# Twelve output-gate pieces and the scan's gate projected between the steps of the triangular inverses, LayerNorm beside the scan

## What is computed

```python
z = h @ w_in
c_in, q, k, v, zg, b_raw, a_raw, gate_c, gate_d = split_cols(z, IN_SPLITS)
u = c_in[..., :512] * sigmoid(c_in[..., 512:])
u = causal_depthwise_conv(u, conv_dw_w) + conv_dw_b          # 31 taps
y_conv = silu(layer_norm(u, gain, bias)) @ w_conv_out
q, k, v = silu(causal_depthwise_conv([q, k, v], gdn_conv_w))  # 4 taps
q, k = l2_normalize(q) * 64 ** -0.5, l2_normalize(k)         # per head
o = gated_delta_rule(q, k, v, beta, g)                       # chunks; (I + L)^-1 per chunk
y_delta = (rms_norm(o, gdn_norm_gain) * silu(zg)) @ w_gdn_out
y = sigmoid(gate_c) * y_conv + sigmoid(gate_d) * y_delta
return y @ w_out
```

## Time and profile before

| | us |
|---|---|
| median of 3 runs | 907.82 |
| lowest and highest | 902.79, 908.47 |
| profiled execution, its time | 912.77 |
| its span | 911.0 |
| TensorE busy in the span | 800.3 (88%) |
| VectorE, ScalarE, GpSimd busy | 565.3, 474.7, 269.3 |
| first VN of the scan begins at | 291.53 |
| last gate piece ends, yc begins at | 427.4, 429.0 |

### The profile page before, as it was taken

The page is one execution under the profiler, slowest core; times in us unless marked ns, Lnnn a source line. Parts: engine busy times, 40 slices in busy tenths (PEclk is TensorE's granted clock), DMA queues, the critical chain, the costliest instruction groups (busy, mean ns, idle before and its releaser), DMA issues.

```text
span 911.0 us, 11270 instructions
## 1 busy us (share of the span) xinstructions
PE 800.3 (88%) x4126; PEld 615.0 (68%) x4126; DVE 565.3 (62%) x753; ACT 474.7 (52%) x660; POOL 269.3 (30%) x172
## 2 busy tenths in 40 slices
PE   4999985968689999999999983999999999999940
PEld 3788864867689788767874562677777777777730
DVE  4278989976733244320241236598888988888826
ACT  6224543355253333346211232588888888888823
POOL 2244415011420222337450002143534444342100
PEclk9999988988777899999999975899999999999975
DMA  8842222000000112224406146499999999899206
GB/s 238 277 139 93 92 93 93 0 1 1 1 1 2 37 57 75 110 93 177 153 20 281 47 157 253 140 353 371 372 379 352 374 352 367 346 347 366 95 16 272
DMA packets 49543, 159.26 MB, mean 175 GB/s; under 512 B 11176, under 2 KB 15288, under 8 KB 41182
## 3 DMA queue, kind: packets, MB, share of 16 engines
q1 hardware_dynamic: 42270, 150.28, 44.3%
q0 software_dynamic: 7232, 8.43, 2.8%
HBM read 152.38 MB, written 23.07 MB: 193 GB/s over the span
## 4 chain that ended last, share of the span: by engine, by line
PE 75%; DVE 11%; ACT 6%; issue 3%; DMA 2%; POOL 1%; SPq 1%; POOLq 0%; DVEq 0%; ACTq 0%
PE bank L397 18%; PE bank L399 17%; PE bank L398 17%; PE bank L741 6%; PE bank L786 3%; DVE arena L1562 3%; DVE bank L1544 2%; PE bank L515 2%; PE bank L644 1%; PE bank L569 1%; PE bank L536 1%; DVE arena L1970 1%; DVE arena L1560 1%; PE bank L546 1%; DMA arena<-in_w_in_dram 1%
## 5 line engine op out<-in xcount | busy, mean ns | idle before, releaser
L1796 DVE TENSOR_TENSOR gu_lo<-wgu,gu_hi 128x2048 fp32r<-128x2048 f32 x64 | 146.4, 2289 | 23.3 <-ACT gu_hi L1406 23.1
L1028 POOL TENSOR_TENSOR w_lo<-arena,w_hi 128x1024 fp32r<-128x1024 f32 x36 | 86.4, 2409 | 187.2 <-ACT w_hi L1151 187.2
L1406 ACT ACTIVATE gu_hi<-wgu 128x2048 fp32r<-128x2048 f32 x64 | 122.2, 1911 | 20.7 <-DMA wgu<-in_w_expert_up_dram 10.9
L397 PE MATMUL bank<-h_hi,w_hi 128*128 128x512 f32 x288 | 117.2, 407 | 4.2 <-DVE arena L1562 4.2
L398 PE MATMUL bank<-h_lo,w_hi 128*128 128x512 f32 x288 | 114.8, 399 | 0.0
L399 PE MATMUL bank<-h_hi,w_lo 128*128 128x512 f32 x288 | 114.8, 399 | 0.0
L1107 POOL DMA_INDIRECT arena<-h_rows,row_idx x32 | 80.4, 2512 | 106.7 <-DVE row_idx L1867 88.7
L397 PE MATMUL bank<-gu_hi,heT_hi 128*96 128x512 f32 x256 | 103.9, 406 | 2.5 <-DVE heT_lo L1891 1.9
L399 PE MATMUL bank<-gu_hi,heT_lo 128*96 128x512 f32 x256 | 102.2, 399 | 0.0
L398 PE MATMUL bank<-gu_lo,heT_hi 128*96 128x512 f32 x256 | 101.5, 397 | 0.0
L1113 POOL DMA_INDIRECT y_rows<-arena,row_idx x32 | 40.6, 1269 | 182.9 <-ACT arena L1445 182.9
(11 more groups left out here) (306 smaller groups left out, 1443.1 us busy)
## 6 DMA issues: line engine op xcount, KB each, us to landing
wgu<-in_w_expert_gate_dram SPq DMA_DIRECT2D x32, 1024.0 KB, 9.2
wgu<-in_w_expert_up_dram SPq DMA_DIRECT2D x32, 1024.0 KB, 19.0
wd<-in_w_expert_down_dram SPq DMA_DIRECT2D x32, 1024.0 KB, 14.1
arena<-in_w_in_dram SPq DMA_DIRECT2D x8, 2048.0 KB, 8.5
arena<-in_x_dram SPq DMA_DIRECT2D x8, 512.0 KB, 8.0
arena<-in_w_in_dram SPq DMA_DIRECT2D x4, 1024.0 KB, 10.6
y_rows<-arena SPq DMA_DIRECT2D x8, 512.0 KB, 10.2
arena<-in_w_out_dram SPq DMA_DIRECT2D x2, 2048.0 KB, 11.6
```

The source lines that it names most:

```text
L397: pe.matmul(o, wh, xh, start=first, stop=False)
L1028: gp.tensor_tensor(as_raw(w_lo[pslot(s)], s), raw(s), as_raw(w_hi[pslot(s)], s).bitcast(F32), ALU.subtract)\
L1406: act.activation(gu_hi[j % 2][:, :, ks, :], wgu[j][:, :, ks, :], ACT.Copy)\
L1796: TT(gu_lo[j][:, :, ks, :], wgu[j][:, :, ks, :], gu_hi[j % 2][:, :, ks, :].bitcast(F32), ALU.subtract)\
```

## The change

- **Order of the chunks**: gate_d's two come before zg, then gate_c's. FIRST_GATE is gate_d's first piece, so from there on two slots hold the parts. zg is projected like the others, features on the partitions (zgT), and no longer as tokens.
- **Sums of squares** of q's and k's heads: ScalarE squares the transposed activations, TensorE multiplies each 128 x 128 block with two columns of ones (head_sums, 4 matmuls per call, 8 calls) into a bank "ss" that is held until both recursions are done. The transposes of q and eight reductions of VectorE go.
- **gate_d** (8 pieces): projected among prep, row_copies and pairs of the low group. ScalarE copies each out of its bank into one of two stages, SP stores it to DRAM (h2T_keep, 256 KB each). After the scan SP reads all 2 MB back, and ScalarE takes the sigmoids (gate_sig) among the branch_hi.
- **zg** (4 pieces) among the joins of low, **gate_c** 0 to 3 among those of high, gate_c 4 to 7 in the scan, one per chunk, behind VN.
- **LayerNorm**: the mean behind OV(0), the variance behind OV(1); VectorE subtracts in chunk 0 and has the reciprocal and the four products in chunk 2, between the state's update and the reading of OV(2); ScalarE squares in chunk 1 and takes silu in chunk 3.
- **own_blocks and the recursion** keep their running sum and product in the bank "ss" instead of SBUF. The taps: 14 ahead of the heads instead of 28, 2 per head in both groups, the rest around own_blocks. gb has four buffers instead of two.
- **Output**: silu(zg) is multiplied behind the transposes (gated), with the norm's gain in the same operation, instead of ahead of them; the last chunk's transposes come behind yc(1); o_lo is made by VectorE instead of GpSimd.
- **Loads**: wco and wgo into the ring slots, as gate_c's chunks are used up; wo1 behind QS(3), wo0 once wco is used up. The row-picking constant is made ahead of kdec's scaling.

```diff
@@ TensorE
+            def head_sums(n):
+                if n == 0:
+                    begin("ss", None)
+                    held.append(jobs["ss"][0])
+                b = bank[jobs["ss"][0]]
+                wait(pe, "sq_ready", n + 1)
+                for c in range(NT):
+                    o = (n // NP) * SC + c * H + 2 * (n % NP)
+                    ins = pe.matmul(b[:, o:o + 2], sq[n % 2][:, c * P:(c + 1) * P], head_of, start=True, stop=True)
+                tell(ins, "ss_mm")
+            def gate(g, m):
+                proj(f"g{'cd'[g]}{m // NP}", m % NP, ("gate", g, m), ("gate_ready", (1 - g) * KT + m + 1), "gate_mm")
...
+            gate(1, 0)
+            gate(1, 1)
+            prep(0)
+            prep(1)
+            gate(1, 2)
+            prep(2)
+            prep(3)
+            for p in range(NP):
+                wait(pe, "silu_ready", 2 * NP + p + 1)
+                tok_tr(vT, p, ("vtok", p), ("vtok_ready", p + 1), "vtok_tr")
+            gate(1, 3)
+            row_copies(0, range(NPR // 2))
+            gate(1, 4)
+            row_copies(0, range(NPR // 2, NPR))
+            prep(4)
+            prep(5)
+            gate(1, 5)
+            prep(6)
+            prep(7)
+            gate(1, 6)
             for b in dw_bank:
+                held.remove(b)
                 used[b] = ("dw_done", CF)
             first_T(low)
             row_copies(1, range(NPR // 2))
             pairs_X(low)
             row_copies(1, range(NPR // 2, NPR))
+            gate(1, 7)
+            pairs_D(low)
+            zg_piece(0)
+            pairs_U(low)
+            join_X(low, 2 * SB)
+            zg_piece(1)
+            join_D(low, 2 * SB)
...
+            join_X(low, HP)
+            zg_piece(2)
+            join_D(low, HP)
+            first_T(high)
+            zg_piece(3)
+            pairs_X(high)
+            gate(0, 0)
+            pairs_D(high)
+            gate(0, 1)
+            pairs_U(high)
+            join_X(high, 2 * SB)
+            gate(0, 2)
+            join_D(high, 2 * SB)
+            join_X(high, HP)
+            gate(0, 3)
+            join_D(high, HP)
@@ the scan on TensorE
                 end(ins, ("VN", c), "scan_mm")
-                gate()
+                gate(0, 4 + c)
...
                 if c > 0:
                     o_tr(c - 1)
-                gate()
+                if c == 0:
+                    b = begin("mean", ("xc_ready", CF))
...
+                if c == 1:
+                    b = begin("var", ("sd_ready", 1))
@@ SyncE
+            def spill(n):
+                for i in range(spilled[0], spilled[0] + n):
+                    wait(sp, "gate_ready", i + 1)
+                    sp.dma_start(h2T_keep[:, i * T:(i + 1) * T], stage[i % NSTG]).then_inc(S[f"st_g{i % NSTG}"], 16)
+                spilled[0] += n
...
+                if n == cidx["zg"]:
+                    spill(2)
+                if n == cidx["gc0"]:
+                    spill(4)
+                if n == cidx["gc1"]:
+                    spill(2)
                 wait(sp, *lo_done((n - 1) * NPC - 1))
                 load(n)
@@ ScalarE
+            def gate_d(m):
+                wait(act, f"st_g{m % NSTG}", 16 * (m // NSTG))
+                tell(act.activation(stage[m % NSTG], ready(act, ("gate", 1, m))[:], ACT.Copy), "gate_ready")
+                hi_part(FIRST_GATE + 2 + m)
...
+            pairs_X(low)
+            gate_d(7)
+            first_U(1)
+            zg_out(0)
+            pairs_U(low)
+            join_X(low, 2 * SB)
+            zg_out(1)
+            join_T(low, 2 * SB)
@@ VectorE
+                own_acc = bank[jobs["ss"][0]][:, 0:HG * SB].rearrange("p (a s) -> p a s", s=SB)
...
+            def gated(c):
+                src = ready(v, ("oT", c)).rearrange("p (f n) -> p f n", f=NP)
+                tell(STT(out=oTc[c], in0=src, scalar=gng, in1=zgT[:, :, c * P:(c + 1) * P], op0=ALU.mult, op1=ALU.mult),
+                     "oT_ready")
...
+                if c == 2:
+                    v.wait_ge(S["sd_ready"], 1)
+                    link(v.reciprocal(lnm, lnv))
+                    v.wait_ge(S["lsq_ready"], CF)
+                    for i in range(CF):
+                        TT(acc[:, i, :], acc[:, i, :], lnm, ALU.mult).then_inc(S["xc_ready"], 1)
                 src = ready(v, ("OV", c))
```

More of the change, by code:

```diff
@@ L142, in hybrid_layer @@
         BP = CF * P
-        b_hi = [parts(f"b_hi{i}", R_ZG + 2 * i * BP, CF, P) for i in range(2)]
-        b_lo = [parts(f"b_lo{i}", R_ZG + (2 * i + 1) * BP, CF, P) for i in range(2)]
+        b_hi = [parts(f"b_hi{i}", R_QK + 2 * i * BP, CF, P) for i in range(2)]
+        b_lo = [parts(f"b_lo{i}", R_QK + (2 * i + 1) * BP, CF, P) for i in range(2)]
         ab_hi = parts("ab_hi", R_ZG + D + T, KT, 2 * H)
@@ L453, in _ @@
                 tok_tr(kT, p, ("ktok", p), ("ktok_copied", p + 1), "tok_tr")
+            head_sums(2)
+            head_sums(3)
             for f in range(NP):
                 proj("v", f, ("qkv", 2 * NP + f), ("tap_done", 2 * NP + f + 1), "qkv_mm")
[L456 to L487, removed]
+                if f >= NP - 2:
+                    head_sums(NP + 2 * (f - NP + 2))
+                    head_sums(NP + 2 * (f - NP + 2) + 1)
             def prep(h):
@@ L494, in prep @@
                 for c in range(NT):
[L495 removed]
+                    ins = pe.matmul(b[:, c * P:(c + 1) * P], gb[h % GRP][:, c, :], triu, start=True, stop=True)
                 end(ins, ("G", h), "G_mm")
@@ L925, in _ @@
                 sp.dma_start(x1[:, c, :], xv[c]).then_inc(S[f"ld_x{c}"], 16)
+            wait(sp, "b_lo", KT)
+            load(cidx["wo0"])
             wgd = a["w_expert_gate"][0].rearrange("(g j) (p k) n -> g j p k n", j=UN, k=KT)
@@ new lines, in _ @@
+            decay(1)
+            gate_d(2)
+            decay(2)
+            decay(3)
+            gate_d(3)
+            gate_d(4)
+            decay(4)
+            decay(5)
+            gate_d(5)
+            decay(6)
+            decay(7)
+            first_U(0)
+            gate_d(6)
+            act.wait_ge(S["dw_done"], CF)
+            first_T(low)
+            pairs_X(low)
[4 more added lines that the diff above has]
+            join_X(low, 2 * SB)
@@ new lines, in _, with gate_c @@
+            zg_out(1)
+            join_T(low, 2 * SB)
+            join_X(low, HP)
+            zg_out(2)
+            first_T(high)
+            def gate_c(m):
+                tell(act.activation(sig[0][:, m, :], ready(act, ("gate", 0, m))[:], ACT.Sigmoid), "gate_ready")
+                s = FIRST_GATE + 2 + KT + NP + m
+                if s <= LAST_PIECE:
+                    hi_part(s)
+            zg_out(3)
+            pairs_X(high)
+            gate_c(0)
+            gate_c(1)
+            pairs_U(high)
@@ L1311, in _ @@
+            join_X(high, 2 * SB)
+            gate_c(2)
+            join_T(high, 2 * SB)
+            join_X(high, HP)
+            gate_c(3)
             act.wait_ge(S["U64_ready"], H)
             wait(act, "D_mm", 2 * H)
-            gates = [(g, m) for g in range(2) for m in range(KT)]
-            def gate(upto):
-                while gates and len(gates) > 2 * KT - upto:
-                    g, m = gates.pop(0)
-                    tell(act.activation(sig[g][:, m, :], ready(act, ("gate", g, m))[:], ACT.Sigmoid), "gate_ready")
-                    s = FIRST_GATE + 2 + g * KT + m
-                    if s < LAST_PIECE:
-                        hi_part(s)
```

373 lines of the change are left out of this document (185 added, 188 removed).

## The result

| | before | changed |
|---|---|---|
| median of 13 runs each, us | 909.41 | 901.02 |
| lowest and highest | 902.79, 912.17 | 899.29, 906.04 |
| span of the profiled execution | 911.0 | 902.3 |
| its granted clock, mean | 0.916 | 0.934 |

The ratio is 0.9924, with an interval from 0.9902 to 0.9946: the change makes the kernel 0.8% faster, 6.9 us by the ratio, where the forecast was 14.0. In the two profiled executions w_out begins at 474.08 and at 466.16, so 7.9 us of the 8.7 between the spans arise ahead of it, and 0.8 behind it.

The account below looks back on a forecast made before the run. TensorE was taken to carry three quarters of the wait chain. Scan start at 340 us (317 + 18 + 5), plus 74, puts yc at 414; less 0.9, gain 14.0: 893.8 against 907.82, range 877 to 909.

Parts of the forecast that it names:

- v's first piece at 128: Before the heads: v's first projected piece waits for conv(7), ending at 128.02, instead of beginning at 122.42; 5.6 us lost.
- Head sums 0.9 a call: q's head sums on TensorE: 4 two-column matmuls per call cost 0.9 us, 3.5 for four calls.
- Waits before the scan, 18: Between 128 us and the scan: TensorE's remaining waits in heads, own_blocks, first_T, joins and U64, with a little for banks: 18 us.
- The low clock before the scan: Up to the scan: half clock costs 1.6 us at v's first piece and 5 for three restarts of 1.7.
- VN(0) at 340: Start of the scan: 317 us without a wait, plus 18 waits and 5 low clock, against 291.53 before.
- VN to VN 17.9, 18.9, 24.2: Scan chunks 0, 1 and 2: time between successive VN starts in us, against 21.0 in the kernel before.
- the third rival: Up to and in the scan: 14 more half-clock restarts than counted, at 1.7 us each, add 24: 918 us; chance 0.08.
- Last part 13.1: Scan's end, from VN(3) to yc: VN, a piece from half clock, QS, OV, transposes, gate and b_lo take 13.1 us.
- From yc on, 0.9: After the scan: kernels alike but for 0.5 us for one late b_hi and 0.4 for o_tr(3).
- the gain is eaten: Rival: eight places where engines interlock cost 1 us more each; gain about 6, time 902 to 912 us; chance 0.22.
- Slower, by the clock: Rival: the sixteen pieces and four of the scan begin at half clock behind small matmuls, adding 24: 918 us; chance 0.08.
- the filled TensorE runs dense: Rival: half the waits before the scan, clock never low, chunk 2's chain hidden; gain 36 us, time 872; chance 0.15.

Follow-up runs that it names:

- copies first: ScalarE's copies of U and of the joins put ahead of zg's and gate-c's copies in the changed kernel: 895.83 us, ratio 0.9852 to the kernel before.
- taps earlier: 20 instead of 14 taps ahead of the heads in the changed kernel: 897.15 us, ratio 0.9866 to the kernel before.
- filler: Useless matmuls, 8 and 4, added ahead of the first joins of size 32 and 64 in the changed kernel: 898.21 us, ratio 0.9866 to the kernel before.
- the filler: Useless matmuls added ahead of VN(1), VN(2), VN(3): 6 each in the kernel before, 903.46 us; 12, 6, 36 in the changed kernel, 895.5 us.

## Why the prediction was half right

The direction and the place of each gap came out; the size did not. I take the steps in the prediction's order.

- **v's first piece at 128.** Measured 128.10, freed by conv(7), after a wait of 3.2. Right.
- **Head sums 0.9 a call, taken from VN's row.** They took 0.84. Right: a matmul with two columns costs as much as one with 64 (0.21 and 0.22). That the width of the weights sets this, as I assumed, no run tried.
- **Waits before the scan, 18.** They came where I had put them: own_blocks(0) 2.1 (2.5 foretold), first_T 4.5 (4.9, by the taps), before the joins 1.8 and 0.9 in the low group and 0.5 and 0.9 in the high one (2 and 1 in each), U64 0.6 (0.6); own_blocks(1) itself took 3.60 (4). But the sum is 12.6, so this term was 5.4 too large, above all in the heads (1.2 instead of 3.2), before the high group's first join, and in the little for banks, which didn't come.
- **The low clock before the scan, 1.6 for v and 5 for three restarts.** This is the step that failed. The stretches lose up to 14.7, not 6.6, and TensorE's busy time is 7.4 above my sum (201.4 against 194). A restart isn't a piece's 1.7 alone: the small matmuls between the wait and the piece run at half speed as well (join_X of 64: 2.82 at 328.65, with the copies first 2.00; and first_T: 3.67 at 234.88, with the taps earlier 1.75). Copies first and filler price the part at the high group's joins and in chunk 0 at about 4.
- **VN(0) at 340.** Measured 342.06: 7.4 more busy and 5.4 less idle nearly cancel. The agreement is luck in part, and the other profiles show how wide it is: with the same code up to there, the way from v's first piece to VN(0) took 214.0, 213.8, 212.6, 212.4, 210.1 and 209.9.
- **VN to VN 17.9, 18.9, 24.2.** Measured 19.2, 20.9, 23.6. In chunk 0 the copies-first kernel, whose VN(0) is at full clock, has 17.6, so the 17.9 stands and the 1.3 beyond it are clock. For chunks 1 and 2 I took over the 21.0 of the kernel before, and these contain a piece at the half clock, 7.18 instead of 5.58: with the filler they fall to 19.4 there. So my two sums had charged 1.6 each for the clock (two of the 3 restarts in the scan that the third rival names), and without it they are 17.3 and 22.6; the changed kernel with the filler has 18.0 and 21.9. What the clock really took is 2.9 in chunk 1 (behind 3.10 us of waiting VN took 1.7 more, 3.65, and its piece 1.2 more, 6.73 from start to start) and 1.6 in chunk 2 (behind 2.31 the piece took 7.15). What I left out is that VN itself runs at half speed behind a wait.
- **Last part 13.1.** Measured 13.3, from 405.73 to yc at 419.07. Right in sum only: VN(3) took 3.64 instead of 1.8, for the same reason, and the rest 1.6 less than counted (the piece 6.72 instead of 7.2, no wait for the first b_lo). From VN(1) on I had charged three pieces, 4.8; the filler prices the clock there at 6.5.
- **From yc on, 0.9.** From 419.07 to 466.16 it is 47.1, before 45.1: 2.0. VectorE's o_lo was costed at nothing, as beside product groups of 12 matmuls. It is beside GpSimd's b_lo that it costs: 3.25 instead of 1.29, and 1.4 on TensorE. In four parts the wait falls by 0.8; that the time falls with it the runs don't resolve, and what the rest is stays open.
- **Loads, stores and low parts at nothing.** No wait of TensorE on a load or a w_lo stands in the trace between 128 and 466. Right by the trace; no run tried it.

Sum of the misses: 2.1 (VN(0)) + 1.3 + 2.0 - 0.6 + 0.2 + 1.1 = 6.1 of the 14.0; left are 7.9, what the starts of w_out show. The low clock stands in it with the larger part of the 7.4 before the scan, 1.3 in chunk 0, 1.3 in chunk 1 and 1.8 at VN(3); terms that I had put too high (5.4 of idle time, 1.6 in the last part) hide about half of this. The time was so within the range, at the edge of the part that I gave to *the gain is eaten* (a gain of 6, and 902 to 912). Its mechanism is not what was found: not eight interlocks of 1 us, but for the most part one cause in several places, the clock. *Slower, by the clock* had the right cause and too many places: pieces between long runs of 512-column matmuls didn't restart (0.98 from 128 to 228), those behind small matmuls with a wait mostly did.

Against *the filled TensorE runs dense* I held that before the clock fell amid busy joins. That reading was too short: TensorE had waits of 1.1 and 0.8 us there, and in the changed kernel, where the waits at the high group's joins go, the clock stays up through the same joins (1.00 from 328 to 345 in four profiles of four). The Trainium skill, "TensorE: Matmul & The Clock Gate", Part 1, says that sustained work lifts the clock; the traces agree once the waits are filled. It also reports a kernel whose many short idles between groups of matmuls made the clock swing; the waits of up to 1.6 us at VN, clock 0.92 with them and 1.00 without, agree with that.

The Trainium skill, "SBUF — State Buffer", section "Who interferes with whom", is borne out in both directions: VectorE's 8.24 instead of 3.60 beside GpSimd, and GpSimd's 3.25 instead of 1.29 beside VectorE. I had applied it to own_blocks, and not to o_lo.

What stays open: from 264 to 290 us the clock was 0.80 to 0.87 in five profiles with the change's order of ScalarE and 1.00 in three, with the same waits before the join. So a wait among small matmuls isn't always followed by the low clock, and there the cause that I name is not shown; what decides wasn't found. Nor is it shown how much each of the four stretches before the scan contributes: only those at the joins and at first_T were changed by themselves, and in the latter the wait and the clock went together.

## What to carry to other kernels

A wait that you find on TensorE, ahead of small matmuls, can have two prices: its length, and the half clock over what comes behind it. Look in the rows whether a stretch that you take over already holds the second, and price it for the small matmuls as for the piece behind them. Where such a wait can't be removed, a few matmuls into the bank that is overwritten next can take the second price away (0.7% in the kernel before, for three lines). When work moves beside a chain, ask at which instruction of the queue it stands: the same 5.85 us of VectorE cost 6.4 behind the state's update and nothing behind VN's copy.

## What the runs showed of the hardware

- The clock stood at its lower level behind waits of only 0.9 to 3.1 us among small matmuls (from 328 to 345 the mean was 0.75 with a wait of 0.9, VN took 3.65 behind one of 3.10). I had looked for it behind the long waits.
- The same code in the same stretch (264 to 290 us) ran at 0.80 in two profiled executions and at 1.00 in three, worth about 4 us: v's first piece to VN(0) took 214.0 and 213.8 in the former, 209.9 and 210.1 in two of the latter.
- A two-input operation of VectorE in SBUF and one of GpSimd hold each other up, in both directions: own_blocks(1) 8.24 instead of 3.60, b_lo 3.25 instead of 1.29. One short state update in the scan (64x256, 0.42 alone) took 2.46 at 373.40 beside a low part of GpSimd. No matmul waited for the state there, but VN(2) then waited 2.31 for what stands behind it in VectorE's queue; I estimate from the rows that 0.7 of the 2.0 reached it.
